# Paged sample attention: keys turned in 32x32 blocks by VectorE, scores as 32x32-tiled products, softmax by half sequences out of PSUM

## The reference, cut to what matters

```python
kp = cache_k[layer, page_table].reshape(B, past, DIFF_HEADS, 2, DIFF_DK).astype(jnp.float32)
vp = cache_v[layer, page_table].reshape(B, past, DIFF_HEADS, DIFF_DV).astype(jnp.float32)
...
s_past = jnp.einsum('bqhmd,bkhmd->bhmqk', q, kp) * DIFF_SCALE + rel_bias_for(rel_bias, n_past)[None, :, None]
s_new = jnp.einsum('bqhmd,bkhmd->bhmqk', q, k.astype(jnp.float32)) * DIFF_SCALE + rel_bias_for(rel_bias, n_new)[None, :, None]
s_new = jnp.where(n_new >= 0, s_new, -jnp.inf)
a = jax.nn.softmax(jnp.concatenate([s_past, s_new], axis=-1), axis=-1)
p = a[:, :, 0] - lam * a[:, :, 1]
return (jnp.einsum('bhqk,bkhe->bqhe', p[..., :past], vp)
        + jnp.einsum('bhqk,bkhe->bqhe', p[..., past:], v.astype(jnp.float32)))
```

## Time and profile before

| what | value |
|---|---|
| times of three runs | 1261.54, 1261.58, 1271.03 us; median 1261.58 us |
| profiled execution: span | 1259.8 us |
| mean granted TensorE clock | 0.925 |
| busy in the span: PE, DVE, ACT, POOL | 1038.3, 584.6, 490.0, 254.2 us |
| paged block | 421.5 to 816.2 us |
| DMA packets, bytes | 106820, 195.21 MB |

### The profile page before, as it was taken

One profiled execution on the slowest core, in us unless ns is written; L12 is line 12 of the kernel. 1 busy time (PEld: TensorE's weight loads), 2 busy tenths in 40 slices (PEclk: granted clock), 3 DMA queues, 4 the chain that ended last, 5 costly groups with the idle time before them and its releaser, 6 DMA issues. The chain is left out here.

```text
span 1259.8 us, 27242 instructions
## 1 busy us (share of the span) xinstructions
PE 1038.3 (82%) x9055; PEld 868.5 (69%) x9055; DVE 584.6 (46%) x1430; ACT 490.0 (39%) x1383; POOL 254.2 (20%) x399
## 2 busy tenths in 40 slices
PE   4999999999999487879878887467788836777998
PEld 4999999997999466556655654155667625664886
DVE  4755522302222134443443443277878458868221
ACT  5644314613424223333333432156767345533110
POOL 0000000000000222343434341222211159800000
PEclk9999999999999799999999998558999967787999
DMA  5312332212111699999999999530000052102221
GB/s 169 93 38 95 106 122 80 82 34 76 53 49 49 215 386 338 385 387 387 387 387 387 387 387 169 148 111 9 17 10 13 1 175 74 51 26 69 97 89 60
DMA packets 106820, 195.21 MB, mean 155 GB/s; under 512 B 14406, under 2 KB 48652, under 8 KB 106732
## 3 DMA queue, kind: packets, MB, share of 16 engines
q1 hardware_dynamic: 85716, 126.03, 30.8%
q0 software_dynamic: 20480, 67.13, 14.3%
q10 hardware_dynamic: 536, 0.89, 0.2%
HBM read 174.41 MB, written 19.60 MB: 154 GB/s over the span
## 5 line engine op out<-in xcount | busy, mean ns | idle before, releaser
L843 POOL DMA_DIRECT2D vraw<-in_cache_v x256 | 137.6, 537 | 667.7 <-issue 663.8
L512 PE MATMUL pz<-wh,xTh 128*128 128x256 f32 (+1 forms) x864 | 248.7, 288 | 0.0
L512 PE MATMUL pz<-wh,xTl 128*128 128x256 f32 (+1 forms) x864 | 244.3, 283 | 0.0
L512 PE MATMUL pz<-wl,xTh 128*128 128x256 f32 (+1 forms) x864 | 244.2, 283 | 0.0
L925 PE MATMUL pk<-ident,kraw 128*128 128x128 f32 x1024 | 136.7, 291 | 57.0 <-DMA kraw<-in_cache_k 54.0
L925 PEld LDWEIGHTS pk<-ident,kraw 128*128 128x128 f32 x1024 | 121.8, 150 | 70.9 <-DMA kraw<-in_cache_k 62.0
L863 DVE COPY kt<-pk 128x512 f32<-128x512 f32 x128 | 82.9, 687 | 183.1 <-PE pk L925 182.1
L512 PEld LDWEIGHTS pz<-wh,xTh 128*128 128x128 f32 (+1 forms) x864 | 160.6, 186 | 1.6 <-issue 1.2
L512 PEld LDWEIGHTS pz<-wh,xTl 128*128 128x128 f32 (+1 forms) x864 | 160.7, 186 | 0.0
L512 PEld LDWEIGHTS pz<-wl,xTh 128*128 128x128 f32 (+1 forms) x864 | 160.5, 186 | 0.0
L643 DVE SCALAR_TENSOR_TENSOR wl<-wraw,nw,wh 128x256 fp32r<-128x256 f32 x112 | 52.3, 482 | 117.1 <-ACT wh L358 116.2
(11 more groups left out here) (241 smaller groups left out, 1857.5 us busy)
## 6 DMA issues: line engine op xcount, KB each, us to landing
kraw<-in_cache_k SPq DMA_DIRECT2D x256, 256.0 KB, 9.6
vraw<-in_cache_v POOLq DMA_DIRECT2D x256, 256.0 KB, 5.7
wraw<-in_w_in SPq DMA_DIRECT2D x14, 1024.0 KB, 5.6
out<-nat SPq DMA_DIRECT2D x32, 128.0 KB, 1.8
xb<-in_x_prompt SPq DMA_DIRECT2D x7, 512.0 KB, 3.6
xr<-in_x_prompt SPq DMA_DIRECT2D x7, 512.0 KB, 3.5
out<-xr SPq DMA_DIRECT2D x7, 512.0 KB, 2.6
val_d<-nat SPq DMA_DIRECT2D x16, 128.0 KB, 1.8
```

The source lines that it names most:

```text
L512: ins = pe.matmul(z_at(u)[0:r, 0:CB], a[:, k, P * i:P * i + r], b[:, c % 2, k, :], start=(n == 0), stop=(n == 3 * KT - 1))
L843: pool.dma_start(vraw[:, g % VR, n, :], cache_v.rearrange("a n p h d -> (a n) p (h d)")[bass.ds(page, 1)] .rearrange("o p c -> (o p) c")). ...
```

## The change

The paged block is written anew, and a few constants with it. Its unit is now a *chunk* of four groups, half a sequence; there are 16 chunks (`NCH`), and all loops are unrolled.

- Keys: DVE turns a whole group by one `transpose` from `kraw` to `kx` in SBUF (128x2048, in 32x32 blocks; two buffers). The 16 transposes on PE, the four `pk` tiles in PSUM and the copies on ACT and DVE are gone.
- Scores: 64 products per group of a 32-row, 32-column stationary (`qz`, zero where a row is another set's) with 128 moving columns, on 16 tiles of the array (four row groups by four column groups); each is again two matmuls in the machine. They add up in `pS_c`, one PSUM tensor of four banks that holds a chunk.
- Softmax per chunk: DVE takes the maximum over 2048 columns of `pS_c`, ACT the exponential of 128x2048 out of `pS_c` into `pr`. `pS_c` exists once, so the scores of the next chunk wait for `exp_done`.
- Probabilities: four transposes per group instead of one (L972), copied by ACT; values as before (L986) with six instead of eight buffers. The two halves of a sequence are joined by weights (`top`, `coefficients`, a product with `spread`, `select`, eight matmuls in `totals`); the result goes through `ods` and a DMA to `od_d` in DRAM, and the next block loads it again.
- Order: the bias products stand first on PE, and DVE's first turned keys stand behind them. SP issues the `skew` DMAs behind the fifth key group instead of behind the last. POOL waits for `band_out` before group 4.

```diff
 @block.sync
 def _(sp):
-    load_keys(0, True)
-    with sp.Fori(1, NB) as kb:
-        load_keys(kb, False)
-    sp.wait_ge(band_out, 1)
-    for h in range(H):
-        sp.dma_start(skew[h:h + 1].rearrange("o (q x) -> o q x", q=P),
-                     band[h:h + 1, :].unsqueeze(1).to_broadcast([1, P, 384])).then_inc(c_in, 16)
+    for g in range(NG):
+        if g >= KR:
+            sp.wait_ge(kx_done, g - KR + 1)
+        for n in range(GRP):
+            page = sp.value_load(pages[0:1, GRP * g + n:GRP * g + n + 1], min_val=0, max_val=POOL - 1)
+            sp.dma_start(kraw[:, g % KR, n, :],
...
+        if g == KR:
+            sp.wait_ge(band_out, 1)
+            for h in range(H):
+                sp.dma_start(skew[h:h + 1].rearrange("o (q x) -> o q x", q=P),
+                             band[h:h + 1, :].unsqueeze(1).to_broadcast([1, P, 384])).then_inc(c_in, 16)
     sp.wait_ge(c_in, 16 * (NCONST + H))
     for n in range(3):
         sp.wait_ge(nat_stored[n], all_stored[n])
+    sp.wait_ge(od_st, 16 * NB)
...
 @block.gpsimd
+    for g in range(NG):
+        if g >= VR:
+            pool.wait_ge(pv_done, pv_upto(g - VR))
+        if g == VR - 2:
+            pool.wait_ge(band_out, 1)
...
 @block.scalar
+    act.activation(pr[:].rearrange("p (n i r) -> p i n r", i=4, r=32),
+                   pS[:, :].rearrange("p (i n r) -> p i n r", i=4, r=32), ACT.Exp,
+                   bias=nmx[:, c:c + 1], accum_out=ls[:, c:c + 1])\
+       .then_inc(exp_done, 1)
...
 @block.tensor
+    def scores(c, g):
+        t = c * CG + g
+        pe.wait_ge(kx_done, t + 1)
         if g == 0:
+            if c % 2 == 0:
+                pe.wait_ge(qz_done, c // 2 + 1)
+            if c:
+                pe.wait_ge(exp_done, c)
+        for j in range(4):
+            for i in range(4):
+                rows = slice(32 * i, 32 * i + 32)
+                for h in range(H):
+                    ins = pe.matmul(pS[32 * h:32 * h + 32, 512 * i + P * g:512 * i + P * (g + 1)],
+                                    qz[rows, c // 2 % 2, h, j, :],
+                                    kx[rows, t % 2, :, P * h + 32 * j:P * h + 32 * j + 32],
+                                    start=(j == 0), stop=(j == 3), tile_position=(32 * i, 32 * h))
+        ins.then_inc(sc_done, 1)
...
+    biases()
     pe.wait_ge(band_out, 1)
+    for c in range(NCH + 1):
+        for g in range(CG):
+            if c < NCH:
+                scores(c, g)
+            if c >= 1:
+                turn_probs(c - 1, g)
+                if g >= 1:
+                    values(c - 1, g - 1)
...
 @block.vector
+    def turn_keys(t):
+        dve.wait_ge(k_in[t % KR], 64 * (t // KR + 1))
+        if t >= 2:
+            dve.wait_ge(sc_done, t - 1)
+        dve.transpose(kx[:, t % 2, :, :].rearrange("p n x -> p (n x)"),
+                      kraw[:, t % KR, :, :].rearrange("p n x -> p (n x)")).then_inc(kx_done, 1)
...
+    dve.tensor_tensor(band[:], negp[:], ptb[0:H, 0:384], ALU.add).then_inc(band_out, 1)
+    dve.wait_ge(band_out, 1)
+    for c in range(NCH + 1):
+        ended = c >= 1 and (c - 1) % 2
+        for g in range(CG):
+            if c < NCH:
+                turn_keys(c * CG + g)
...
+        if c < NCH:
+            if c % 2:
+                new_keys(c // 2)
+            maxima(c)
+        if ended:
+            select((c - 1) // 2)
+            store_out((c - 1) // 2)
```

More of the change, by code:

```diff
@@ L763, in hymba_kernel @@
[L763 to L773, removed]
@@ L917, in _ @@
+                store(NB - 1)
             @block.tensor
             def _(pe):
-                def turn_keys(kb, g, h):
-                    if h == 0:
-                        pe.wait_ge(k_in[g % KR], kb * 128 + 64 * (g // KR + 1))
-                    if not (first(kb) and g == 0):
-                        pe.wait_ge(kt_act if h < 2 else kt_dve, kb * (2 * G) + 2 * (g - 1) + h % 2 + 1)
-                    for n in range(GRP):
-                        ins = pe.transpose(pk[h][:, n * PAGE:(n + 1) * PAGE],
-                                           kraw[:, g % KR, n, h * P:(h + 1) * P], ident[:])
-                    ins.then_inc(kt_done, 1)
@@ new lines, in turn_probs @@
+                def turn_probs(c, g):
+                    n = pt_no[("turn", c, g)]
+                    free_pt(n)
+                    if g == 0:
+                        pe.wait_ge(exp_done, c + 1)
+                    if g < CG:
+                        for m in range(GRP):
+                            at = (GRP * g + m) * P
+                            ins = pe.transpose(ptb[:, m * P:(m + 1) * P], pr[:, at:at + P], ident[:])
+                    else:
+                        ins = pe.transpose(ptb[0:NS, 0:P], pn[:], ident[:])
+                    ins.then_inc(pt_done, 1)
@@ new lines, in values @@
+                def values(c, g):
+                    v = pv_no[(c, g)]
+                    t = c * CG + g
+                    pe.wait_ge(pt_out, pt_no[("turn", c, g)] + 1)
+                    if g == 0 and c:
+                        pe.wait_ge(o_out, c)
+                    if g < CG:
+                        pe.wait_ge(v_in[t % VR], 64 * (t // VR + 1))
+                        for n in range(GRP):
+                            ins = pe.matmul(po[32 * n:32 * n + 32, :], pT[:, v % 2, 32 * n:32 * n + 32],
+                                            vraw[:, t % VR, n, :], start=(g == 0),
+                                            stop=(g == CG - 1 and (n > 0 or c % 2 == 0)), tile_position=(0, 32 * n))
+                    else:
+                        ins = pe.matmul(po[0:32, :], pT[0:NS, v % 2, 0:32], vn[:], start=False, stop=True,
+                                        tile_position=(0, 0))
+                    ins.then_inc(pv_done, 1)
@@ L1170, in hymba_kernel @@
             ob = sb(st, "ob", [P, W])
+            od_s = sb(st, "od_s", [NS, W])
+            od_in = sem("od_in")
             mix = sb(st, "mix_b", [P, W])
```

544 lines of the change are left out of this document (244 added, 300 removed).

## The result

The changed kernel takes 1383.65 us (three runs, 1382.75 to 1386.54) against 1261.58 us: 1.094 times as long, with a 95% interval of 1.089 to 1.099. The profiled execution has a span of 1381.9 us at a mean granted clock of 0.845. The direction of the forecast holds, the size does not: 1275 was said, with 1340 as the upper end.

A forecast was written before the change was run, and what follows sets the result against it. Loads at 387 GB/s were taken to bound the paged block, which loses time at its ends. 1259.8 + 10.8 (start and tail) + 3 (missed pace) + 1.8 (span to median) = 1275 us; range 1247 to 1340.

The forecast's parts named there:

- part 2: The seam of a chunk: 16.6 us a chunk, below the loads' 21.7; 3 us booked for chunks missing the pace.
- part 1: Keys and scores in the steady state: a group's scores 1.1 us, PE 2.8 us per group against 5.42.
- fourth rival: Instructions come late in PE's written-out list: 0 to 66 us of waiting, 1305 us in all; chance 0.06.
- rival of slow transposes: DVE's key transposes take 5.7 us each or stall value loads: a chunk of 27 us, 1355 us; chance 0.08.
- PE becomes the bound: Tiles not running together, or a low clock, make a chunk 26.2 us: 1335 us; chance 0.20.
- the case's own range: Around the forecast, 1260 to 1292 us: `band_out` five us early or fifteen late, the tail 27 to 39.
- Part 3: Start of the block: `skew` writes hold the DMA engines some 25 us; the last keys land near 795.
- Part 4: Tail of the block: 33 us of work behind the last keys, block end at 827 against 816.2.

## Why the prediction was wrong

**What bounds the kernel before**, and that the removed transposes and copies bring nothing by themselves: right. With `skew` mended, that kernel gains at its end alone.

**The step that failed** is the sum of a chunk in part 2: 16.6 us, 20.5 at a clock of 0.71, "below 21.7". It was 28.7 us. Two terms of it are wrong: the scores of part 1, too small, and the pieces of PE's list, which stand outside the sum in the fourth rival.

**Part 1**, the scores: "If 16 tiles work together as four do, that is 8 x 0.11 + 0.2 = 1.1 us". A group's scores were 1.90 to 2.81 us. The 16 tiles do work together (if only four did, a group would take 3.5 us at full clock, by the same part). What I left out is that each product has a weight load of its own and that both are instructions: 256 in a group's scores where transposes and scores before had 96, because the stationary there stood for 128 rows and here for 32. Three rows at full clock give an estimate of each term: 64 matmuls of 128 columns took 1.07 us, 128 of them 1.90, and 128 of 256 columns 2.75. By these the columns are 0.85 us of the 1.90 (8 x 0.11 was said), the 128 pairs of load and matmul 0.8 (nothing was said), and what is left 0.24 (0.2 was said). At the low clock the same sums (1.52, 2.81 and 4.52) give 1.7, 0.9 and 0.2: the columns double, the pairs hardly change. The rule of the Trainium skill that the prediction weighed among its rivals ("TensorE: Matmul & The Clock Gate", Part 1, starts never closer than about 25 ns) doesn't hold here: 128 matmuls in 1.90 us are 15 ns apart. DVE's transpose was right (64 of 2295 ns, for 2.3 us). With half of the products the loads came to 379 GB/s beside the same transposes, and value pages landed 6.0 us after their issue (5.7 before), so the rival of slow transposes fell; the trap of the Trainium skill, "SBUF — State Buffer", section "SBUF: two separate sides", didn't show.

**Part 2** booked 3 us for chunks that miss the pace, "with 0 and 70 as the ends"; it was 105. The seam was about right (maximum 2.3, exponential 1.95 to 2.2, some 5.8 us of waiting), and a shorter maximum left a chunk at 28.3 us. Against the 20.5 us for a clock of 0.71 (0.74 was measured), scores are 4.5 us of the difference (10.4 against 4 x 1.1 at that clock), waits on issue 2, the other products some 1.5. But scores alone don't explain the pace: with 32 columns they take 6.7 us a chunk, and the chunk is 28.7 us all the same. The term that decides is that of the pieces, 4.6 a chunk at 6.2 us, which the sum has at nothing.

**The rivals.** "PE becomes the bound" came closest, with 1335 us; its reasons are tiles one after the other, which the runs exclude, or a low clock, which lengthens the products but doesn't set the pace. The fourth, late instructions, was priced at 0 to 66 us, by what a piece takes of one DMA engine (1.1 us), and taken alone; "fetched ahead they cost nothing" had no row behind it. It was real, and it acts as a floor that takes back what other edits save. I had set scores and pieces apart; both come from one number, the instructions that the change adds. (1275 plus half of 66 is 1308, not 1305, and the case's own range by its two terms is 1264 to 1296, not 1260 to 1292; neither changes the outcome.)

**Part 3**, the start: right in kind, though all of it came earlier. The band was ready at 439.9 (445 was said), SP issued the `skew` writes at 446.67, and 80 GB/s moved from 460 to 482. That PE stands there for instructions, and not for keys alone, was not foreseen; the price was near the 25 us foreseen, 20 us by the run with `skew` out of DRAM.

**Part 4**, the tail: 31.9 us from the start of the last turning of keys (901.6) to the end of the block, 27 to 39 said.

What stays open is how the gain of fewer products divides between weight loads and pieces, since no run changed the pieces with the same products; a loop on PE would, and it wasn't tried. Two runs narrow it, from 500 to 780. With 32 columns and all products a chunk takes 28.7 us, with half of the products 22.6, though the score products of a chunk are only 1 us apart (6.7 and 5.7). Waits on issue are 3.2 us of the 6.1, and the other products, at a lower clock, 2.4. So the pieces outweigh the loads of weights there.

## What to carry to other kernels

Count TensorE's instructions, and not its columns alone, when a change cuts products into smaller tiles and writes out the loops: here four times as many score products at a quarter of the array each, in a list of 4.6 pieces per chunk, cost 105 us, and the same columns in wider products, with the orders fitted to them, won most of it back. Where several different edits to a chain each give less than they take away, look at what the time turned into; here it was one row, the wait on issue. And look at what fills a slow stretch before moving it: four small DMAs out of one partition each cost some 20 us in either kernel.

## What the runs showed of the hardware

512 writes of 1536 B out of four partitions of SBUF, with key pages between them, held the DMA engines for some 20 us (0.87 busy at 28 GB/s from 456 to 474); out of DRAM they leave no wait on issue over 3.7 us at that place. While the slow ones ran, TensorE's next instructions did not come for 24 us. At the start of the block, beside the loads, 256 instructions of TensorE came every 6.2 to 6.5 us; where its list needs a 16 KB piece only each 13 us, it waited for none. A product of 32x32 tiles had, besides its columns, 6 to 7 ns for the pair of load and matmul at either clock (an estimate from 0.8 and 0.9 us for 128). A TensorE that is given filler work in its idle time had a clock of 0.84 instead of 0.74, and the kernel was no faster for it.
